# Dividing the prompt weights before their transposition in mixer A

## What is computed

```python
logits = q @ k_sel * HEAD_DIM ** -0.5 + bias          # masked where a key is not selected
p = jax.nn.softmax(logits, axis=-1)                   # exp(logits - max) / sum
o = p @ v_sel
```

## Time and profile before

| | us |
|---|---|
| median of 3 runs | 2319.15 |
| lowest and highest | 2312.81, 2322.72 |
| the profiled execution, its own time | 2322.22 |
| its span, first to last instruction | 2320.4 |
| TensorE busy (share of the span) | 2247.8 (97%) |
| VectorE busy | 1151.6 (50%) |
| GpSimd busy | 1033.5 (45%) |
| ScalarE busy | 404.8 (17%) |
| mean granted clock of TensorE | 0.985 of full |

### The profile page before, as it was taken

One profiled execution on the slowest core, in us unless ns is written; L12 is line 12 of the kernel. 1 busy time (PEld: TensorE's weight loads), 2 busy tenths in 40 slices (PEclk: granted clock), 3 DMA queues, 4 the chain that ended last, 5 costly groups with the idle time before them and its releaser, 6 DMA issues.

```text
span 2320.4 us, 39568 instructions
## 1 busy us (share of the span) xinstructions
PE 2247.8 (97%) x14691; PEld 2020.3 (87%) x14691; DVE 1151.6 (50%) x1863; ACT 404.8 (17%) x826; POOL 1033.5 (45%) x625
## 2 busy tenths in 40 slices
PE   7999999999998899999999999999999999999997
PEld 6999989958766588999999999999997689999997
DVE  4545522478885546555522555542266465555311
ACT  3000000141454412000000101000015420100002
POOL 3555555423201035555555555555551055555552
PEclk9999999999998999999999999999999899999998
DMA  5434363544203432333233333323351033333231
GB/s 126 92 80 110 79 155 89 102 88 116 42 2 110 135 85 73 83 87 84 75 86 84 85 87 83 81 74 87 90 154 28 1 79 83 84 82 80 80 84 60
DMA packets 378041, 196.32 MB, mean 85 GB/s; under 512 B 66531, under 2 KB 374476, under 8 KB 377932
## 3 DMA queue, kind: packets, MB, share of 16 engines
q1 hardware_dynamic: 366108, 180.79, 31.6%
q10 hardware_dynamic: 11552, 13.71, 2.1%
q0 software_dynamic: 288, 0.56, 0.1%
HBM read 192.23 MB, written 11.64 MB: 88 GB/s over the span
## 4 chain that ended last, share of the span: by engine, by line
PE 62%; DVE 2%; ACT 0%; issue 0%; DVEq 0%; ACTq 0%
PE psum L607 17%; PE psum L610 11%; PE psum L606 11%; PE psum L608 11%; PE psum L609 9%; DVE XS L1560 1%; PE psum L841 1%; PE psum L871 1%; PE psum L857 1%; PE psum L837 1%; DVE squares L1593 0%; PE psum L1017 0%; PE psum L1016 0%; PE psum L627 0%; PE psum L692 0%
## 5 line engine op out<-in xcount | busy, mean ns | idle before, releaser
L544 POOL CAST WSP<-WST 128x1024 fp32r<-128x1024 f32 (+1 forms) x305 | 312.8, 1025 | 1221.8 <-PE psum L610 1004.8
L546 POOL TENSOR_TENSOR WSP<-WST,WSP 128x1024 fp32r<-128x1024 f32 (+1 forms) x305 | 708.7, 2324 | 24.4
L607 PE MATMUL psum<-XS,WSP 128*128 128x512 f32 x1672 | 659.1, 394 | 0.0
L606 PE MATMUL psum<-XS,WSP 128*128 128x320 f32 x1672 | 521.3, 312 | 9.7 <-DVE XS L1560 4.3
L610 PE MATMUL psum<-XS,WSP 128*128 128x320 f32 x1672 | 522.7, 313 | 0.0
L608 PE MATMUL psum<-XS,WSP 128*128 128x320 f32 x1672 | 519.9, 311 | 0.0
L609 PE MATMUL psum<-XS,WSP 128*128 128x256 f32 x1672 | 474.7, 284 | 0.0
L609 PEld LDWEIGHTS psum<-XS,WSP 128*128 128x128 f32 x1672 | 315.4, 189 | 71.2
L606 PEld LDWEIGHTS psum<-XS,WSP 128*128 128x128 f32 x1672 | 321.8, 192 | 12.1 <-DVE XS L1560 5.2
L610 PEld LDWEIGHTS psum<-XS,WSP 128*128 128x128 f32 x1672 | 321.8, 192 | 0.0
L607 PEld LDWEIGHTS psum<-XS,WSP 128*128 128x128 f32 x1672 | 314.5, 188 | 0.4
(11 more groups left out here) (320 smaller groups left out, 2584.0 us busy)
## 6 DMA issues: line engine op xcount, KB each, us to landing
WST<-in_ffn_w_gate SPq DMA_DIRECT2D x168, 256.0 KB, 3.9
WST<-in_ffn_w_up SPq DMA_DIRECT2D x168, 256.0 KB, 4.0
WST<-in_ffn_w_down SPq DMA_DIRECT2D x192, 224.0 KB, 3.5
WST<-in_a_w_in SPq DMA_DIRECT2D x28, 256.0 KB, 4.7
kv0A<-in_cache_kv SPq DMA_DIRECT2D x48, 128.0 KB, 2.3
kv2A<-in_cache_kv SPq DMA_DIRECT2D x48, 128.0 KB, 2.2
WST<-in_b_w_in SPq DMA_DIRECT2D x20, 256.0 KB, 4.1
kscr<-in_cache_idx SPq DMA_DIRECT2D x128, 32.0 KB, 2.0
```

Of the source, the lines that this page charges most:

```text
L544: nc.gpsimd.tensor_copy(WSP[s][:, 0, 0:width], WST[s][:, 0:width]).then_inc(w_hi, 1)
L546: nc.gpsimd.tensor_tensor(WSP[s][:, 1, 0:width], WST[s][:, 0:width], WSP[s][:, 0, 0:width].bitcast(F32), ALU.subtract).then_inc(w_split, 1)
L606: mm(front, high, x[:, 0, 0:FRONT], start=first, stop=False)
L607: mm(split, high, x[:, :, FRONT:TOK], start=first, stop=False)
```

## The change

Mixer A's prompt stage gets mixer B's way. One function `prompt_attention(L, ...)` per engine serves both mixers, with the number of sink columns `SINK[L]` 0 for A and 2 for B. In mixer A the reciprocals and the scaling of the exponentials are done on VectorE in every unit, ahead of the transposition; the transposed row scales, their copies, the products and `otok` are gone; high and low parts come out of PSUM; the order on TensorE is logits, values, transposition. GpSimd's first split of the projection out waits for the last scaling (`pn_set`) in place of the last logits. ScalarE's loop gets a call that counts a step of the search in the units listed in `SIGN_UNITS`, which is empty. Mixer B's instructions stay as they were.

```diff
@@ GpSimd
-            pool.wait_ge(MS["A"]["qk_ps"], NQT * GRP)
+            pool.wait_ge(MS["A"]["pn_set"], 2 * NQT * GRP)
@@ TensorE
-            def paged_prompt_attention(m, ms, aend):
-                units = [(r, i, g) for r, i in enumerate(ORDER["A"]) for g in range(GRP)]
+            def prompt_attention(L, m, ms, aend):
+                units = [(r, i, g) for r, i in enumerate(ORDER[L]) for g in range(GRP)]
...
-                    if u > GRP and g == 1:
-                        pe.wait_ge(ms["r_set"], 2 * r)
-                    masked, w = i > 0, min(nk, 2 * P)
+                    masked, w = L == "A" and i > 0, min(nk, 2 * P)
...
-                def row_scales(r, i):
-
-                    pe.wait_ge(ms["ri_set"], r + 1)
-                    for g in range(GRP):
-                        for n in range(KVH):
-                            ins = mm(PS[1][n * HD:(n + 1) * HD, g // 4, g % 4 * P:(g % 4 + 1) * P],
-                                     m["ri"][:, i, n, g:g + 1].to_broadcast([P, HD]), ident[:, :], start=True, stop=True)
-                        if g % 4 == 3:
-                            ins.then_inc(ms["r_ps"], 1)
...
                     for n in range(KVH):
-                        pe.wait_ge(ms["p_set"], 2 * u + n + 1)
-                        out, free = turned_place("A", u, n, nk)
+                        pe.wait_ge(ms["pn_set"], 2 * u + n + 1)
+                        out, free = turned_place(L, u, n, nk)
...
-                for u, (r, i, g) in enumerate(units):
-                    more = u + 2 < len(units)
-                    transposed(u)
-                    if g == GRP - 1:
-                        row_scales(r, i)
-                    elif more:
-                        logits(u + 2)
-                    if u:
-                        values(u - 1)
-                    if g == GRP - 1 and more:
-                        logits(u + 2)
+                for u in range(len(units)):
+                    if u + 2 < len(units):
+                        logits(u + 2)
+                    if u:
+                        values(u - 1)
+                    transposed(u)
@@ ScalarE
-                def scales(r):
-                    for h in range(2):
-                        act.wait_ge(ms["r_ps"], 2 * r + h + 1)
-                        if r:
-                            act.wait_ge(ms["ot_evac"], 2 * r)
-                        fn(m["otok"][:, 4 * h:4 * h + 4, :].rearrange("p g t -> p (g t)"), PS[1][:, h, :], ACT.Copy)\
-                            .then_inc(ms["r_set"], 1)
...
+                def high_part(r, h):
+                    i = ORDER[L][r]
+                    act.wait_ge(ms["pv_ps"], GRP * r + 4 * h + 4)
+                    fn(XH[:, 4 * h:4 * h + 4, i * P:(i + 1) * P], bank[6 + h].rearrange("p (g t) -> p g t", g=4), ACT.Copy)\
+                        .then_inc(ms["oh_set"], 1)
...
+            def later_counts(u):
+
+                if u in SIGN_UNITS:
+                    count(FOUND + 1 + u)
+
+            prompt_attention("A", m, ms, later_counts)
@@ VectorE
-                def row_scales(r):
...
-                    nc.vector.reciprocal(ri, rs).then_inc(ms["ri_set"], 1)
...
-                        tt(o, bank[6 + h], o, ALU.mult).then_inc(ms["o_evac"], 1)
...
-                        tt(XL[s], o, XH[s].bitcast(F32), ALU.subtract).then_inc(ms["ot_evac"], 1)
...
                     nc.vector.reciprocal(m["ri"][:, i, :, g], m["rs"][:, i, :, g]).then_inc(ms["ri_set"], 1)
                     dve.wait_ge(ms["ri_set"], u + 1)
                     for n in range(KVH):
-                        p = m["p"][:, u % 2, n, 0:key_range("B", i)[1]]
+                        p = m["p"][:, u % 2, n, 0:key_range(L, i)[1]]
                         ts(p, p, m["ri"][:, i, n, g:g + 1], None, ALU.mult).then_inc(ms["pn_set"], 1)
...
-                return -2 ** 31 if 1 <= k <= FOUND else 0
+                return -2 ** 31 if k in SIGNED else 0
...
-SINK = 2
-STRIP_B = 2 * P + SINK
+SINK = {"A": 0, "B": 2}
+STRIP = {L: 2 * P + SINK[L] for L in "AB"}
...
-BITS, FOUND = 32, 7
+BITS, FOUND, SIGN_UNITS = 32, 7, ()
+SIGNED = (*range(1, FOUND + 1), *(FOUND + 1 + u for u in SIGN_UNITS))
```

More of the change, by code:

```diff
@@ L303, in bass_hybrid_step @@
                       "dotsP_ps", "dotsS_ps", "rP_set", "rS_set", "r_usedS", "r_usedP", "s_evac", "pmask_set", "maskS_set", "selb_in",
-                      "cm_used", "seek_set", "count_set", "qbd_clear", "r_ps", "r_set", "o_evac", "newS_ps", "newS_set", "riS_set") + tuple(f"kv_in{s}{c}" for s in range(KV_SLOTS)
+                      "cm_used", "seek_set", "count_set", "qbd_clear", "newS_ps", "newS_set", "riS_set") + tuple(f"kv_in{s}{c}" for s in range(KV_SLOTS)
                                                                    for c in range(KT_GROUPS)),
-                "B": ("pn_set", "kv_in", "ptnS_evac", "esS_in", "esS_set")}
+                "B": ("kv_in", "ptnS_evac", "esS_in", "esS_set")}
         MS = {L: {k: sem(k + L) for k in both + only[L]} for L in "AB"}
@@ L756, in logits @@
                     for n in range(KVH):
-                        for k, part in enumerate((m["stripH"][:, n], strip_low("A", n))):
-                            mm(PS[u % 2][:, n, nk - w:nk], m["identr"][:, :], part[:, g, 2 * P - w:2 * P],
+                        for k, part in enumerate((m["stripH"][:, n], strip_low(L, n))):
+                            mm(PS[u % 2][:, n, nk - w:nk + SINK[L]], m["identr"][:, :], part[:, g, 2 * P - w:STRIP[L]],
                                start=k == 0 and not masked, stop=False)
@@ L795, in values @@
                     r, i, g = units[u]
[L796 to L804, removed]
@@ L820, in paged_prompt_attention @@
[L820 to L831, removed]
-                        pe.wait_ge(ms["p_set"], 2 * (u - 1))
-                    if u == 0:
-                        pe.wait_ge(ms["strip_set"], KVH)
-                    for n in range(KVH):
-                        for k, part in enumerate((m["stripH"][:, n], strip_low("B", n))):
-                            mm(PS[u % 2][:, n, 0:nk + SINK], m["identr"][:, :], part[:, g, 2 * P - nk:STRIP_B],
-                               start=k == 0, stop=False)
-                    for n in range(KVH):
-                        h = slice(n * HD, (n + 1) * HD)
-                        ins = mm(PS[u % 2][:, n, 0:nk], m["qT"][h, g, i * P:(i + 1) * P], m["kT"][h, k0:k0 + nk],
-                                 start=False, stop=True)
-                    ins.then_inc(ms["qk_ps"], 1)
-                turned = turned_counts("B")
-                def transposed(u):
-                    r, i, g = units[u]
-                    nk = key_range("B", i)[1]
-                    for n in range(KVH):
-                        pe.wait_ge(ms["pn_set"], 2 * u + n + 1)
-                        out, free = turned_place("B", u, n, nk)
-                        if free >= 0:
-                            pe.wait_ge(ms["pt_evac"], turned[free] if nk <= 2 * P or n else turned[free] - 1)
-                        for k in range(nk // P):
-                            ins = nc.tensor.transpose(out[:, k * P:(k + 1) * P], m["p"][:, u % 2, n, k * P:(k + 1) * P],
-                                                      ident[:, :])
-                        if n or nk > 2 * P:
-                            ins.then_inc(ms["pt_ps"], 1)
-                def values(u):
-                    r, i, g = units[u]
-                    k0, nk = key_range("B", i)
@@ L872, in values @@
                                      m["kvtok"][:, k0 // P + k, KVW + n * HD:KVW + (n + 1) * HD],
-                                     weights_of("B", u)[:, n, k, :], start=k == 0, stop=k == nk // P - 1)
+                                     weights_of(L, u)[:, n, k, :], start=k == 0, stop=k == nk // P - 1)
                     ins.then_inc(ms["pv_ps"], 1)
@@ L1335, in window_prompt_attention @@
-            def window_prompt_attention(m, ms):
-                units = [(r, i, g) for r, i in enumerate(ORDER["B"]) for g in range(GRP)]
-                turned = turned_counts("B")
-                def exps(u):
-                    r, i, g = units[u]
-                    nk = key_range("B", i)[1] + SINK
+                    nk = key_range(L, i)[1] + SINK[L]
                     act.wait_ge(ms["nm_set"], u + 1)
@@ L1715, in window_prompt_attention, with prompt_attention @@
-            def window_prompt_attention(m, ms, between, after):
-                units = [(r, i, g) for r, i in enumerate(ORDER["B"]) for g in range(GRP)]
+            def prompt_attention(L, m, ms, between, after):
+                units = [(r, i, g) for r, i in enumerate(ORDER[L]) for g in range(GRP)]
                 def factors(u):
@@ L2087, in _ @@
             steps.mark(tt(m["strip"][:, :, :, 2 * P], m["nsink"][:, :, :], m["es"][:, :, :], ALU.subtract))
-            steps.mark(nc.vector.memset(m["strip"][:, :, :, 2 * P + 1:STRIP_B], MASK))
+            steps.mark(nc.vector.memset(m["strip"][:, :, :, 2 * P + 1:STRIP["B"]], MASK))
```

(2 more changed lines are left out.)

122 lines of the change are left out of this document (24 added, 98 removed).

## The result

| | before | after |
|---|---|---|
| median of 5 runs each, same chip | 2317.73 | 2333.18 |
| lowest and highest | 2312.81, 2322.72 | 2329.88, 2333.63 |
| profiled execution, its own time | 2322.22 | 2333.18 |
| its span | 2320.4 | 2331.4 |
| VectorE, ScalarE busy | 1151.6, 404.8 | 1167.7, 402.8 |

The ratio is 1.0059, with the interval [1.0043, 1.0074]. The changed kernel measured again, unedited, beside 29 further runs of the kernel before gave 1.0028 [1.0015, 1.0041] (experiment e5). Three edits that leave the stage's length as it is, within 2 us, gave 1.0028, 1.0052 and 1.0040. The mean of the five is 1.0041, some 9.6 us; this is the number that the rest explains.

What follows compares the result with a forecast made beforehand. The prediction tied the sample stage to the end of the last prompt logits, with VectorE becoming the prompt stage's bound. The 4.6 us later logits, all else nothing, were added to the median 2319.15: 2323.8 us, "same", range 2315 to 2333.

Steps and rivals of the forecast that it cites:

- VectorE per unit, the factors: Mixer A's prompt stage: reciprocal and scalings add 1.01, 0.87, 0.73 and 0.59 us per unit at 512 to 128 columns.
- Rivals 3 and 4: Wide scalings on VectorE cost in proportion to width, 2328.6 us, 8%; or the same at any width, 2321.3 us, 7%.
- The sum to the mask: VectorE without idle from the second maximum takes 102.4 us in total, so the mask is done 4.9 us later.
- The tail: Three TensorE rounds behind the mask, at the 1.2 GHz level, end the last prompt logits at 716.2, 4.6 us later.
- Rival 2: Fast tail: TensorE's clock is at 2.4 GHz when the mask is done, so +1.1 us, 2320 us; 17%.
- TensorE leaves the prompt stage some 3 us later: Into mixer A's sample stage: without 3.15 us of row scales, TensorE's later start is hidden behind the page loads.
- the 4.5 to spare: TensorE's slack into the sample stage, from its two waits for page loads, 1.62 and 2.89 us.
- The prediction's own sign of being wrong: Maxima waiting for logits at a low clock in middle tiles, or the last page load not moving like the first.
- Rival 1: TensorE's clock falls in the 384 and 256 key tiles: 2346 us, 10%; in the 256 tile alone 2331, 10%.
- GpSimd's later wait: GpSimd's first split starts at about 719 instead of 711.71; costs nothing, as the projection needing it comes past 813 us.
- The counts: The list of units whose count ScalarE would take is empty: no instruction changes, no cost.
- SyncE's steps of 15.6 us: Page loads of the sample stage: after the last prompt logits, six steps of 15.56 us each follow, unchanged but later.

Runs made afterwards that it cites:

- e1: Changed kernel with idle-time matmuls on TensorE ahead of the transpositions of units 20 to 26, to hold the clock; ratio to the kernel before 1.0015.
- e2: Changed kernel with SyncE loading the second sample's pages after 24 of the 32 prompt logits, not all; ratio to the kernel before 1.0028.
- e10: Changed kernel with SyncE reading the page numbers of samples 1 to 3 before its wait on the prompt logits; ratio to the kernel before 1.0040.
- e6: Changed kernel with GpSimd's wait ahead of its first split put back on the count of prompt logits; ratio to the kernel before 1.0052.
- e7: Kernel before with idle-time matmuls on TensorE in units 20, 25, 26 and 27, meant to hold the clock; ratio to the unedited kernel before 1.0000.
- e9: Kernel before with SyncE reading the page numbers of samples 1 to 3 before its wait on the prompt logits; ratio to the unedited kernel before 1.0000.
- e4: Changed kernel with the scalings of mixer A's prompt weights on GpSimd, reciprocals staying on VectorE; ratio to the kernel before 1.0014.
- e8: Changed kernel with mixer A's scalings on GpSimd and idle-time matmuls on TensorE in units 18 to 26; ratio to the kernel before 1.0006.
- e11: Changed kernel with idle-time matmuls on TensorE in units 20 to 26 and page numbers read ahead on SyncE; ratio to the kernel before 1.0013.
- e12: Changed kernel with mixer A's scalings on GpSimd, idle-time matmuls in units 18 to 26 and page numbers read ahead; ratio to the kernel before 1.0003.
- e3: Changed kernel with mixer A's scalings of prompt weights cut to one column of each tile; ratio to the kernel before 0.9988.

## Why the prediction was right or wrong

By its class the forecast, "same", stands at the border: 1.0059 lies over its 0.5%, 1.0028 under. Its number, 2323.8, was 5 us short of the 9.6 measured, and the median of the first runs, 2333.18, lies just outside the range.

**VectorE per unit, the factors: right.** Line through two rows for the wide scalings: 0.487 and 0.419 predicted, 0.484 and 0.418 measured. Periods 4.18, 3.77, 3.36 predicted; 4.17, 3.77, 3.37 measured. Rivals 3 and 4 fall.

**The sum to the mask: right.** 102.4 us from the second maximum, 102.35 measured.

**The tail: right.** Last logits at 111.1 us from the second maximum, measured 110.95 (711.23 + 0.80 - 601.08), with the clock at 0.50 as taken. Rival 2 falls.

**"TensorE leaves the prompt stage some 3 us later ... less than the 4.6 of the loads and the 4.5 to spare together, so hidden": this is the step that failed**, in three places. TensorE left 4.6 us later, not 3 (first sample keys at +117.04 against +112.42): losing the 3.15 us of row scales won nothing, since the rounds left behind the last logits took 6.1 us, before 5.9 with the row scales among them. Then the low clock went with it into the sample stage, which the prediction had only in the tail, and made 4.6 into 10.2 us by the end of sample 0's values. And the 4.5 to spare was read where the stage ends, at TensorE's waits for pages, while the first thing that a late TensorE delays is the release of sample 0's buffer, with 3.0 us to spare. 10.2 - 3.0 = 7.2 us, against the 7.4 that seq 3 is later. Had the buffer been free, SyncE's own chain, 4.5 us late, would have started that set at about +142.1 (an estimate, 137.61 + 4.5), so the late release adds 2.9 of the 7.4. e1 takes the clock away and gives back 5.4 of these; e2 and e10 show that SyncE's chain ahead of seq 3, made earlier, doesn't bring it back. The prediction's own sign of being wrong came: the first page transfer moved by 4.5 us, the last by 9.0 (+209.06 against +200.06). That the clock fell earlier because VectorE's longer units leave TensorE idle is borne out by e1 (fillers in those gaps) but only for all gaps together.

**Rival 1, the clock falling in the middle tiles: not as priced.** TensorE idled 0.7 to 1.4 us in each late 256-key unit, and the clock held 1.00 until 692, when that tile was nearly done; VectorE still bound the units. The price came behind the mask. The rule of the Trainium skill, TensorE: Matmul & The Clock Gate, section "A second HAM failure mode: psum-queue depth-cycling", which stood beside this rival, speaks of a clock that swings to and fro under short idles; the trace shows one fall and one long stay at 1.2 GHz instead.

**Everything else.** GpSimd's later wait: nothing, by e6 (its first split at +114.7, as the 719 said). The counts: no instruction changed. SyncE's steps of 15.6 us: right, for a profiled execution that was at the short edge of 15.6 to 16.5.

**What stays open.** The sum of the stage, 7.4 us and the scatter of its steps, is not the whole difference of the profiled spans. Over the five executions of the changed kernel that leave its length alone (after, e2, e5, e6, e10) and the three of the kernel before (with e7 and e9), the span differs by 8.8 us: -3.9 up to the second maximum, +8.6 in the stage, +1.1 to B's first maximum, +2.8 in mixer B, +0.2 behind it. Mixer B came in two lengths, 93.5 to 94.7 us or 96.8 to 97.0, with its granted clock over the sample attention lower in the long one (24 us at 0.73 in e4; 28 us at 0.57 in e8). Four of the five had the long one, none of the three; two of the five runs e1, e4, e8, e11 and e12 had it too. B's instructions and their order are the same in all. Whether the clock falls there by the change or by chance, and why the stretch ahead of mixer A is shorter, wasn't settled.

## What to carry to other kernels

Where a stage is fed through a ring of buffers, look at which event releases each slot from the first round on, and take the spare time there; the waits at the end of the chain show only what is left. When an engine becomes the bound ahead of a TensorE stage, price TensorE's clock not only in the units that wait but for the stage behind them, since here the low clock was carried along for 36 us. And an idle third engine may take work at three times its cost (1562 ns against 484) and still be the better place, if the work fits in the unit.

## What the hardware showed unexpectedly

- The clock stayed at 1.2 GHz for some 36 us, 692 to 729, although TensorE was busy 3.5 to 4.0 of 4 us in most windows from 704; in e3 it was back within some 24 us, in e7 it fell in the window behind the last fillers.
- Between two sets of transfers, in which SyncE reads sixteen page numbers into registers, 7.0 us pass, nearly as much as issuing sixteen transfers takes (8.1); with the numbers read ahead 0.5 us are left (e9), so the reading is some 6.5 us, 0.41 each. The Trainium skill, Runtime: NRT & Kernel Launch, section "Instruction fetch mechanics", gives some 200 ns for a register load from memory, by which it would be an estimated 3.2 us; the measured time decides here.
- With GpSimd scaling beside it, one of VectorE's tiny steps grew: the mean of the instruction with two inputs went from 159 to 294 ns (0.16 where GpSimd was idle, up to 0.53), while its neighbours with one input stayed (214 against 215, 154 against 153). Groups by form, changed kernel and e4:

```profile
L1801 DVE SCALAR_TENSOR_TENSOR seekA<-seekA 128x1 int32<-128x1 int32 x24 | 3.8, 159 | 0.8
```

```profile
L1807 DVE SCALAR_TENSOR_TENSOR seekA<-seekA 128x1 int32<-128x1 int32 x25 | 7.3, 294 | 0.8
L1806 DVE TENSOR_SCALAR seekA<-countA 128x1 int32<-128x1 f32 x25 | 5.4, 214 | 0.9
```

In the other direction it was GpSimd that grew: its first 128-column scaling, started 0.1 us behind VectorE's scan of 2.30 us (L1890), took 2.60 us, against 0.59 behind the mask. The Trainium skill, SBUF — State Buffer, section "SBUF: two separate sides", says that VectorE's operations with two SBUF inputs and GpSimd's share a port pair, and that whichever comes second waits for the other's whole instruction. GpSimd's 2.60 us agree. VectorE's tiny step doesn't: it grew by at most 0.4 us and ended while GpSimd's 1.56 us were still running (605.85 + 0.53 against 605.69 + 1.56).
